# A router on unnormed, transposed half blocks, and a first index taken before the softmax

## The chip, the cores and the metric

The kernel runs on one core of a Trainium2 chip. The metric is the device time of one execution in microseconds (us). Before the change it was 1559.31 us, the median of three runs (1558.9 to 1561.21).

## The reference, cut to what matters

One layer of an encoder: 512 tokens of width 1024, two attention branches, an output projection, and a mixture of 32 experts of which each token uses four. All of it is float32. The part that the change touches:

```
x  = x + merged @ w_out
h2 = x * rsqrt(mean(x*x) + eps) * g_ffn
logits = h2 @ w_router + b_router            # (512, 32)
top_vals, top_idx = top_k(logits, 4);  gate = softmax(top_vals)
# each expert: rows h2[tokens of e]; gu = rows @ w_gate_up[e] + b; clamped SwiGLU; @ w_down[e] + b; times gate
x  = x + sum over the experts;  out = rmsnorm(x) * g_final
```

## The kernel before, in words

There is no planner: each engine runs a list of instructions written out by hand, in order, and waits on semaphores. A product in float32 is made of three float32r products: each operand is split into a rounded part ("hi", copied by ScalarE, ACT) and the rest ("lo", subtracted by VectorE, DVE), and TensorE (PE) multiplies hi by hi, hi by lo and lo by hi (L1446 to L1448, one 128x512 product each). The router alone multiplies in plain float32.

**Output projection.** `out_part(n, j)` is six products of quarter `j` of the depth for half block `n`; half block `n` is 512 columns of token block `n // 2`. Half blocks 0 to 3 go through together, then 4 to 7 one after the other. `residual(n)` (L1231, DVE) adds a half block to `xs`. `root(c)` (L890 to L892, ACT) starts the store of block `c` of `xs` to memory, squares it, and takes the root; `norm(c)` (L1237, L1238, DVE) writes the normed block to `xn2`, and `store_rows(c)` (ACT's queue) stores that as rows to gather from.

**Routing.** `h2_transpose` (L1650, PE) turns eight 128x128 tiles of the normed block, ACT and DVE copy four each out of PSUM (`h2T_half` L872, `h2_out` L1245), `router` (L1660, PE) makes the logits. `choose(c)` (L1251 to L1259, DVE) finds the top four and the mask. From the masks PE counts positions (L1686, L1689), DVE makes `posx` (L1307, L1309). `softmax` (L1266 to L1273, DVE) makes the gates in three bfloat16 parts. `serve(n)` (L1318, DVE) writes the one-hot matrix of expert `n`, `slots(n)` (L1701, PE) multiplies it with index and gates, `index(n)` (L931 to L939, ACT) turns that into row numbers and gates, and GpSimd (POOL) gathers the 128 rows (L618). `rows_in` (L1708, PE) transposes them, and ACT (`rows_hi`, L943) and DVE (`rows_lo`, L1324) split them into `XT`.

**Experts.** An expert has twelve 1 MB chunks of weights. For chunk `c`, ACT copies hi (`first_split_hi` L883 or `ex_split_hi` L879), DVE subtracts lo (`ex_split_lo` L1279), PE runs twelve products (`weigh`). Chunks 0 to 3 (gate) of the first expert come ahead of the loop; then each turn of the loop runs chunks 4, 5, `slots` and `rows_in` for later experts, 6, 7, then 0, 1 of the next expert, the transposes of the hidden rows (L1716), 2, 3, and 8 to 11. `sigmoid` (L969, ACT, behind a table load at L972) and `glu` (L1358, DVE) come once per expert; `serve` for the next expert stands behind `glu`. SyncE (SP) issues the loads of chunks, each when its place is free. In the first expert it loads chunks 4 to 7 when the output projection is done, and 8 to 11 when the first gather has landed:

```
sp.wait_ge(wout_ps, 2 * NT)
sp.dma_start(bd[:, :], b_down[0]).then_inc(bd_in, 16)
for c in range(4, 8):
    load_expert(sp, c, 0)
```

## Time and profile before

| what | value |
|---|---|
| median of three runs | 1559.31 us |
| the profiled execution | 1559.76 us, of it the span 1558.0 us |
| PE, DVE, ACT, POOL busy | 97%, 84%, 70%, 17% of the span |
| chain that ended last | PE 93%, DVE 3%, ACT 2%, issue 1% |
| granted TensorE clock, mean | 0.986 |
| DMA over the span | 477.36 MB, mean 306 GB/s |

Busy time is what the hardware profiler recorded of one execution. An engine's idle time costs something only where another engine's last work waits for it; the chain of waits, followed back from the last instruction, tells which engine that is.

### The profile page before, as it was taken

Reading aid. Unit: us, or ns where it says so; the run is one execution under the profiler, and the core shown is the slowest. Engines: PE = TensorE matmul, PEld = TensorE weight load, DVE = VectorE, ACT = ScalarE, POOL = GpSimd, SP = SyncE. Lnnn points to the kernel's source line nnn. Section 1 sums busy time; section 2 is a strip of 40 time slices with the busy share of each in tenths; the row PEclk is TensorE's granted clock in tenths of the full one; section 3 lists DMA queues with packets and bytes.
Section 4 is the critical chain, followed back from the end, with each engine's and each line's share of the span. In section 5 each row is a group of like instructions: output and inputs, shape, how many; then the busy total and the mean of one; then the engine's idle time right before and its main releaser. Section 6 shows DMA issues by size and latency. Waiting matters only on the chain.

```text
span 1558.0 us, 21230 instructions
## 1 busy us (share of the span) xinstructions
PE 1512.6 (97%) x7254; PEld 1240.9 (80%) x7287; DVE 1311.9 (84%) x1021; ACT 1091.1 (70%) x1158; POOL 268.3 (17%) x164
## 2 busy tenths in 40 slices
PE   7999999997999999999999999999999999999997
PEld 6888788886788888888888888888888888888884
DVE  4556587656899999999999999999999999999975
ACT  4344587424787777877777787787777778778772
POOL 6302144100001110111100001202120022002211
PEclk9999999998899999999999999999999999999997
DMA  8330001545999999999999999999999999999972
GB/s 299 122 100 36 1 1 55 200 141 181 378 363 391 385 389 385 379 391 379 375 387 386 386 387 381 388 390 385 376 372 391 386 378 394 387 387 380 388 263 113
DMA packets 131102, 477.36 MB, mean 306 GB/s; under 512 B 9720, under 2 KB 10240, under 8 KB 130976
## 3 DMA queue, kind: packets, MB, share of 16 engines
q1 hardware_dynamic: 117536, 434.79, 72.1%
q0 software_dynamic: 9936, 36.44, 9.1%
q10 hardware_dynamic: 3600, 5.73, 1.1%
q8 instruction: 18, 0.29, 0.1%
q14 instruction: 12, 0.10, 0.0%
HBM read 452.81 MB, written 24.12 MB: 306 GB/s over the span
## 4 chain that ended last, share of the span: by engine, by line
PE 93%; DVE 3%; ACT 2%; issue 1%; DMA 0%; ACTq 0%; SPq 0%; DVEq 0%
PE ps L1446 28%; PE ps L1447 28%; PE ps L1448 28%; PE ps L1708 2%; PE ps L1716 2%; PE ps L1735 2%; PE ps L1494 1%; PE ps L1537 1%; DVE pT_lo L1155 1%; PE ps L1538 0%; ACT probs L754 0%; PE ps L1479 0%; DMA xs<-in_x 0%; DVE split L1068 0%; PE ps L1515 0%
## 5 line engine op out<-in xcount | busy, mean ns | idle before, releaser
L1279 DVE TENSOR_TENSOR chunk_lo<-chunk,chunk_hi 128x2048 fp32r<-128x2048 f32 x384 | 859.3, 2285 | 39.0 <-ACT chunk_hi L879 36.0
L879 ACT ACTIVATE chunk_hi<-chunk 128x2048 fp32r<-128x2048 f32 x378 | 722.6, 1914 | 109.2 <-PE ps L1448 108.1
L1446 PE MATMUL ps<-chunk_hi,XT 128*128 128x512 f32 x1024 | 404.8, 395 | 2.0 <-DVE XT L1324 2.0
L1448 PE MATMUL ps<-chunk_hi,XT 128*128 128x512 f32 x1024 | 400.0, 391 | 0.0
L1447 PE MATMUL ps<-chunk_lo,XT 128*128 128x512 f32 x1024 | 399.9, 391 | 0.0
L644 POOL DMA_INDIRECT sum_rows<-y,idx x31 | 116.4, 3755 | 921.7 <-ACT y L985 833.8
L1446 PEld LDWEIGHTS ps<-chunk_hi,XT 128*128 128x128 f32 x1024 | 192.8, 188 | 41.1 <-DVE XT L1324 2.4
L1448 PEld LDWEIGHTS ps<-chunk_hi,XT 128*128 128x128 f32 x1024 | 192.4, 188 | 40.4
L1447 PEld LDWEIGHTS ps<-chunk_lo,XT 128*128 128x128 f32 x1024 | 192.8, 188 | 38.9
L1446 PE MATMUL ps<-chunk_hi,hidT 128*128 128x512 f32 x512 | 200.4, 391 | 0.0
L1448 PE MATMUL ps<-chunk_hi,hidT 128*128 128x512 f32 x512 | 200.1, 391 | 0.0
L1447 PE MATMUL ps<-chunk_lo,hidT 128*128 128x512 f32 x512 | 200.1, 391 | 0.0
L1446 PEld LDWEIGHTS ps<-chunk_hi,hidT 128*128 128x128 f32 x512 | 96.8, 189 | 21.6 <-issue 1.4
L1447 PEld LDWEIGHTS ps<-chunk_lo,hidT 128*128 128x128 f32 x512 | 96.8, 189 | 20.2
L1448 PEld LDWEIGHTS ps<-chunk_hi,hidT 128*128 128x128 f32 x512 | 96.7, 189 | 20.2
L943 ACT ACTIVATE XT<-ps 128x512 fp32r<-128x512 f32 x64 | 38.2, 599 | 79.3 <-PE ps L1708 54.9
L1068 DVE TENSOR_TENSOR split<-raw,split 128x2048 fp32r<-128x2048 f32 x14 | 37.2, 2660 | 54.2 <-ACT split L694 54.2
L618 POOL DMA_INDIRECT xg<-h_rows,idx x34 | 46.1, 1357 | 150.7 <-ACT idx L937 106.0
L1382 DVE TENSOR_SCALAR hid<-ps 128x1024 f32<-128x1024 f32 x32 | 39.2, 1224 | 29.3 <-PE ps L1448 29.3
L1446 PE MATMUL ps<-hT,split 128*128 128x512 f32 x128 | 50.2, 392 | 0.0
L1448 PE MATMUL ps<-hT,split 128*128 128x512 f32 x128 | 49.9, 390 | 0.0
L754 ACT ACTIVATE probs<-ps,negm 128x512 f32<-128x512 f32 (+2 forms) x64 | 39.4, 616 | 14.9 <-DVE negm L1161 14.5
(272 smaller groups left out, 1900.7 us busy)
## 6 DMA issues: line engine op xcount, KB each, us to landing
chunk<-in_w_gate_up SPq DMA_DIRECT2D x256, 1024.0 KB, 8.8
chunk<-in_w_down SPq DMA_DIRECT2D x128, 1024.0 KB, 7.1
raw<-in_w_in SPq DMA_DIRECT2D x14, 1024.0 KB, 6.8
xs<-in_x SPq DMA_DIRECT2D x8, 512.0 KB, 5.2
w_out<-in_w_out SPq DMA_DIRECT2D x4, 1024.0 KB, 6.8
raw<-in_w_branch_a SPq DMA_DIRECT2D x2, 1024.0 KB, 6.0
raw<-in_w_branch_b SPq DMA_DIRECT2D x2, 1024.0 KB, 6.9
sum_rows<-xs ACTq DMA_DIRECT2D x4, 512.0 KB, 2.6
```

Of the source, the lines that this page charges most:

```text
L618: g.indirect_dma_start(out=xg, out_offset=None, in_=h2buf, in_offset=bass.IndirectOffsetOnAxis(ap=idx[:, col:col + 1], axis=0)).then_inc(g ...
L644: g.indirect_dma_start(out=acc, out_offset=bass.IndirectOffsetOnAxis(ap=idx[:, u:u + 1], axis=0), in_=ysb, in_offset=None, compute_op=ALU. ...
L754: a.activation(probs[:, j % 2, n, 0:w], ps[:, i % 3, 0:w], ACT.Exp, bias=negm[:, j % 2, n:n + 1], accum_out=psum_p[:, j % 2, n:n + 1]).the ...
L879: a.activation(chunk_hi[hi_slot(c, nxt)][:, :], chunk[c][:, :], ACT.Copy).then_inc(ex_hi, 1)
L943: a.activation(XT[:, 0, 4 * half:4 * half + 4, :].rearrange("p k n -> p (k n)"), ps[:, 6 + half, 0:4 * CAP], ACT.Copy).then_inc(xt_hi, 1)
L1068: v.tensor_tensor(split[:, n % NIN_SPLIT, 1, :], raw[:, n % NIN, :], split[:, n % NIN_SPLIT, 0, :].bitcast(F32), ALU.subtract).then_inc(in ...
L1279: v.tensor_tensor(chunk_lo[c][:, :], chunk[c][:, :], chunk_hi[hi_slot(c, nxt, first)][:, :].bitcast(F32), ALU.subtract).then_inc(ex_lo, 1)
L1382: v.tensor_scalar(hid, ps[0:CAP, 2:4, :].rearrange("p t n -> p (t n)"), 8.0, -6.0, ALU.min, ALU.max).then_inc(clip_ready, 1)
L1446: mm(dst, lhsT(0), rhs(0), start=start, stop=False)
L1447: mm(dst, lhsT(0), rhs(1), start=False, stop=False)
L1448: return mm(dst, lhsT(1), rhs(0), start=False, stop=stop)
L1708: last = t_.transpose(ps[:, 6 + k // 4, (k % 4) * CAP:(k % 4 + 1) * CAP], xg[:, k * 128:(k + 1) * 128], ident[0:CAP, 0:CAP])
```

## The change

The router multiplies the unnormed sums `xs`, transposed in half blocks of 512 columns (`x1T`, four places), with router weights that DVE has multiplied once by `g_ffn`; the factor 1/rms of a token is put on the logits in `choose`. The half transposes and half routers stand between the quarter products of half blocks 4 to 7. On ACT the stores of `xs` come behind the roots, and the square of the last block is taken in two halves. The first expert's index is made from a product with two columns (index and one), ahead of the softmax of all four blocks, its gates later by a second product. `slots(2)`, the third expert's index product, stands behind `weigh` of chunk 2, and ACT's `index(2)` behind the splitting of the gathered rows and of chunk 3. The gathered rows are split half by half. On SP, chunks 4 and 5 are loaded behind the output projection, the bias table and chunks 6 to 11 when all rows are stored, and `b_down` last.

```diff
 # SP
             sp.wait_ge(wout_ps, 2 * NT)
-            sp.dma_start(bd[:, :], b_down[0]).then_inc(bd_in, 16)
-            for c in range(4, 8):
-                load_expert(sp, c, 0)
+            load_expert(sp, 4, 0)
+            load_expert(sp, 5, 0)
+            sp.wait_ge(rows_stored, 2 * NT * 16)
             sp.wait_ge(scattered, ADDED)
             sp.dma_start(bias_tab[:, :], bias_parts).then_inc(bias_back, 16)
-            sp.wait_ge(gathered, 16)
-            for c in range(8, 12):
+            for c in range(6, 12):
+                if c == 8:
+                    sp.wait_ge(logits_ps, 2 * NT)
                 load_expert(sp, c, 0)
+            sp.dma_start(bd[:, :], b_down[0]).then_inc(bd_in, 16)
 # ACT
+            act.dma_start(g16[8:16, :], g_ffn.rearrange("l (k p) -> (l k) p", p=128)).then_inc(g_mix_in, 16)
...
+            root(0)
+            store_sums(0)
+            root(1)
+            store_sums(1)
+            x1T_out(0)
+            x1T_out(2)
             store_rows(0)
             store_rows(1)
             act.wait_ge(branch_ps, KD)
             first_split_hi(0)
+            root(2)
+            x1T_out(4)
+            store_sums(2)
+            store_rows(2)
+            half_square(0)
...
+            x1T_out(6)
+            half_square(1)
...
+            store_sums(3)
+            store_rows(3)
             a.activation(warm[:, :], eps[:, :], ACT.Exp)
+            for c in range(NT):
+                top_exp(c)
...
+            act.wait_ge(idx_first, 1)
+            a.activation(f5[:, 0:2], ps[0:CAP, 5, 440:442], ACT.Copy).then_inc(f2_ready, 1)
...
+            a.activation(idx[:, 0:1], f5[:, 0:1], ACT.Identity, bias=s1[:, 0:1]).then_inc(idx_ready, 1)
+            first_split_hi(1)
+            act.wait_ge(idx_done, 1)
...
             act.wait_ge(gates_set, 1)
             index(1, slice(1, 2))
+            act.wait_ge(wout_ps, 2 * NT)
+            first_split_hi(2)
             act.wait_ge(gateT_ps, 1)
             a.activation(gateT[:, :], ps[0:E, 3, :], ACT.Copy).then_inc(gateT_out, 1)
+            act.wait_ge(xt_first, 1)
+            a.activation(XT[:, 0, 0:4, :].rearrange("p k n -> p (k n)"), ps[:, 6, 0:4 * CAP], ACT.Copy).then_inc(xt_hi, 1)
+            rows_hi(1, 1)
+            first_split_hi(3)
+            act.wait_ge(gates_set, 2)
+            index(2, slice(2, 3))
             act.wait_ge(rows_stored, 2 * NT * 16)
             first_split_hi(4)
             first_split_hi(5)
 # DVE
+            dve.wait_ge(late_in, 32)
+            v.tensor_tensor(wr[:, :, :], wr[:, :, :], gcol[:, KD:2 * KD].unsqueeze(2).to_broadcast([128, KD, E]),
+                            ALU.mult).then_inc(wr_scaled, 1)
             for n in range(4):
                 residual(n)
             norm(0)
+            x1T_copy(1)
             norm(1)
+            x1T_copy(3)
+            choose(0)
             residual(4)
+            ex_split_lo(0, 0, first=True)
+            choose(1)
             residual(5)
             norm(2)
+            x1T_copy(5)
             residual(6)
+            choose(2)
             residual(7)
+            x1T_copy(7)
             norm(3)
             choose(3)
...
             serve(0)
+            softmax(0, NT)
+            dve.wait_ge(idx_done, 1)
+            serve(1)
+            ex_split_lo(0, 1, first=True)
+            ex_split_lo(0, 2, first=True)
+            rows_lo(1, 0)
+            rows_lo(1, 1)
+            ex_split_lo(0, 3, first=True)
...
             dve.wait_ge(idx_done, 2)
             serve(2)
 # PE
+            def x1_transpose(n):
+                pe.wait_ge(x1_ready, n + 1)
+                if n >= 2:
+                    pe.wait_ge(x1T_odd if n % 2 else x1T_even, n // 2)
+                for k in range(4):
+                    at = n % 2 * 512 + k * 128
+                    last = t_.transpose(ps[:, n % 2, k * 128:(k + 1) * 128], xs[:, n // 2, at:at + 128], ident[:, :])
+                last.then_inc(x1T_ps, 1)
...
+            out_part(5, 3)
+            out_part(6, 0)
+            router(4)
+            out_part(6, 1)
+            x1_transpose(5)
+            out_part(6, 2)
+            out_part(6, 3)
+            router(5)
+            out_part(7, 0)
+            out_part(7, 1)
+            x1_transpose(6)
+            out_part(7, 2)
+            out_part(7, 3)
+            router(6)
+            x1_transpose(7)
             pe.wait_ge(wout_ps, 2 * NT)
             pe.sem_inc(ex_used, 2)
+            router(7)
...
+            pe.wait_ge(gathered, 16)
+            for k in range(KD):
...
+                if k == 3:
+                    last.then_inc(xt_first, 1)
+            last.then_inc(xt_ps, 1)
             for c in range(4):
+                if c % 2 == 0:
+                    pe.wait_ge(xt_lo, c // 2 + 1)
...
                 weigh(c, c, c, XT, 0, c == 0, c == 3).then_inc(ex_used, 1)
+                if c == 2:
+                    slots(2)
+            pe.wait_ge(f5_ready, 3)
```

## Rows read from the trace of the kernel before

**Rows 1.** Busy time by stretch: engines in order, then PEclk, DMA share, GB/s.

```profile
core 0: us, PE busy (x) PEld busy (x) DVE busy (x) ACT busy (x) POOL busy (x), PEclk, DMA share, GB/s
369.00:396.00 27.00, 12.50 (x112) 11.05 (x111) 21.60 (x61) 15.87 (x33) 3.52 (x2) 0.67 0.78 278
484.00:520.00 36.00, 35.93 (x171) 29.47 (x171) 33.74 (x20) 28.41 (x25) 6.33 (x3) 1.00 1.02 387
```

**Rows 2.** Timeline of PE: start us, us, line, operation, count, [idle before, releaser].

```profile
343.68 0.39 PE L1446 MATMUL ps<-w_out_hi,merged_T_hi 128*128 128x512 f32 x1
...
354.56 1.03 PE L1650 MATMUL ps<-ident,xn_a 128*128 128x128 f32 x8
355.35 0.48 PE L1446 MATMUL ps<-w_out_hi,merged_T_hi 128*128 128x512 f32 x1
...
360.93 1.86 PE L1660 MATMUL ps<-w_router,h2T 128*128 128x32 f32 x16
...
395.91 0.80 PE L1446 MATMUL ps<-chunk_hi,XT 128*128 128x512 f32 x1 [2.01 <-DVE XT L1324]
...
405.78 0.38 PE L1735 MATMUL ps<-bias_tab,pick 128*128 128x512 bf16 x1
...
414.18 0.26 PE L1701 MATMUL ps<-feats,shared 128*128 x4
```

**Rows 3.** Timeline of ACT, the same columns.

```profile
355.86 1.06 ACT L890 ACTIVATE xn_b<-xs 128x1024 f32<-128x1024 f32 x1 [9.40 <-DVE xs L1231]
357.24 0.58 ACT L872 ACTIVATE h2T<-ps 128x512 f32<-128x512 f32 x1
...
384.66 0.28 ACT L937 ACTIVATE idx<-f,s 128x1 int32<-128x1 f32 x1
...
391.60 0.28 ACT L939 ACTIVATE gates<-f,s 128x1 f32<-128x1 f32 x1
...
395.39 3.70 ACT L883 ACTIVATE chunk_hi<-chunk 128x2048 fp32r<-128x2048 f32 x2
...
405.03 1.28 ACT L972 ACT_TABLE_LOAD   x1
...
408.93 1.03 ACT L969 ACTIVATE sig<-ps 128x1024 f32<-128x1024 f32 x1 [2.41 <-PE ps L1448]
```

**Rows 4.** Timeline of DVE, the same columns.

```profile
369.21 0.69 DVE L1231 TENSOR_TENSOR xs<-xs,ps 128x512 f32<-128x512 f32 x1 [0.74 <-PE ps L1448]
...
378.71 0.19 DVE L1251 TENSOR_TENSOR lg<-ps,brt 128x32 f32<-128x32 f32 x1
...
379.72 0.18 DVE L1259 TENSOR_SCALAR mask<-repl 128x32 bf16<-128x32 f32 x1
...
380.86 0.18 DVE L1266 TENSOR_TENSOR shared<-shared,mask 128x32 f32<-128x32 f32 x1
...
382.92 0.69 DVE L1318 TENSOR_TENSOR shared<-iota_all,shared 128x512 bf16<-128x512 f32 x1
...
397.31 4.49 DVE L1279 TENSOR_TENSOR chunk_lo<-chunk,chunk_hi 128x2048 fp32r<-128x2048 f32 x2 [1.46 <-ACT chunk_hi L883]
...
409.99 1.23 DVE L1358 TENSOR_TENSOR sig<-ps,sig 128x1024 f32<-128x1024 f32 x1 [2.66 <-ACT sig L969]
411.13 0.68 DVE L1318 TENSOR_TENSOR shared<-iota_all,shared 128x512 bf16 x1
```

**Rows 5.** Timeline of POOL: the first gather.

```profile
385.83 2.56 POOL L618 DMA_INDIRECT xg<-h_rows,idx  x1 [106.01 <-ACT idx L937]
```

**Rows 6.** DMA issues at 358.88, 373.33, 385.83 and 394.70 us: count, KB, us to landing.

```profile
h_rows<-xn_b ACTq DMA_DIRECT2D x1, 512.0 KB, 2.6
...
h_rows<-xn_b ACTq DMA_DIRECT2D x1, 512.0 KB, 9.3
...
xg<-h_rows,idx POOLq DMA_INDIRECT x1, 5.9
...
xg<-h_rows,idx POOLq DMA_INDIRECT x1, 8.3
```

**Rows 7.** Waits over the whole span: us in total, times, longest.

```profile
PE ps L1458 <- DVE gcol L1060: 4.2, 1, 4.2
```

More of the change, by code:

```diff
@@ L306, in encoder_block @@
         sums_ready = sem("sums_ready")
-        acc_in = [sem(f"acc_in{c}") for c in range(NT)]
         gfin_in = sem("gfin_in")
@@ L865, in _, with x1T_out @@
             wo_split_hi(3)
-            def h2T_half(c):
-                act.wait_ge(h2T_ps, c + 1)
-                if c >= 2:
-                    act.wait_ge(logits_ps, c - 1)
-                a.activation(h2T[:, c % 2, 0:4, :], ps[:, 0, :].rearrange("p (k n) -> p k n", n=128),
-                             ACT.Copy).then_inc(h2T_a, 1)
+            def x1T_out(n):
+                act.wait_ge(x1T_ps, n + 1)
+                if n >= 4:
+                    act.wait_ge(logits_ps, n - 3)
+                a.activation(x1T[:, n % 4, :, :], ps[:, 0, :].rearrange("p (k n) -> p k n", n=128),
+                             ACT.Copy).then_inc(x1T_even, 1)
             def ex_split_hi(i, c, nxt=True):
@@ L1309, in _ @@
             v.tensor_scalar(posx[:, :, :], posx[:, :, :], -1024.0, None, ALU.add).then_inc(route_ready, 1)
-            softmax(3, 4)
             dve.wait_ge(route_ready, 1)
@@ L1343, in _ @@
             v.tensor_copy(items_i[:, 0:1], npass[:, :]).then_inc(items_ready, 1)
-            dve.wait_ge(idx_done, 1)
-            serve(1)
-            for c in range(1, 3):
-                ex_split_lo(0, c, first=True)
             dve.wait_ge(idx_done, 2)
             serve(2)
-            ex_split_lo(0, 3, first=True)
-            rows_lo(1, 0)
-            rows_lo(1, 1)
             dve.wait_ge(items_ready, 1)
@@ L1642, in out_half, with router @@
                     out_part(n, j)
-            def h2_transpose(c):
-                pe.wait_ge(xn2_ready, c + 1)
-                if c:
-                    pe.wait_ge(h2T_a, c)
-                    pe.wait_ge(h2T_d, c)
-                for k in range(KD):
-                    last = t_.transpose(ps[:, k // 4, (k % 4) * 128:(k % 4 + 1) * 128],
-                                        xn2[c][:, k * 128:(k + 1) * 128], ident[:, :])
-                last.then_inc(h2T_ps, 1)
-            def router(c):
-                pe.wait_ge(h2T_a, c + 1)
-                pe.wait_ge(h2T_d, c + 1)
-                if c >= 2:
+            def x1_transpose(n):
[6 more added lines that the diff above has]
+                last.then_inc(x1T_ps, 1)
+            def router(n):
+                c = n // 2
+                pe.wait_ge(x1T_odd if n % 2 else x1T_even, n // 2 + 1)
+                if n == 0:
+                    pe.wait_ge(wr_scaled, 1)
+                if c >= 2 and n % 2 == 0:
                     pe.wait_ge(lg_ready, c - 1)
-                for k in range(KD):
-                    last = mm(ps[:, 2 + c % 2, c * E:(c + 1) * E], h2T[:, c % 2, k, :], wr[:, k, :],
-                              start=(k == 0), stop=(k == KD - 1))
+                for k in range(4):
+                    last = mm(ps[:, 2 + c % 2, c * E:(c + 1) * E], x1T[:, n % 4, k, :], wr[:, n % 2 * 4 + k, :],
+                              start=(n % 2 == 0 and k == 0), stop=(n % 2 == 1 and k == 3))
                 last.then_inc(logits_ps, 1)
@@ L1736, in add_bias @@
                        bias_tab[:, col:col + 512], start=start, stop=False)
-            slots(0)
+            pe.wait_ge(onehot_ready, 1)
+            for c in range(NT):
+                last = mm(ps[0:CAP, 5, 440:442], onehot[:, c, :], feats[:, c, 0, 0:2], start=(c == 0), stop=(c == NT - 1))
+            last.then_inc(idx_first, 1)
+            pe.wait_ge(f2_ready, 1)
+            pe.wait_ge(gates_known, 1)
+            for c in range(NT):
+                last = mm(ps[0:CAP, 5, 450:453], onehot[:, c, :], feats[:, c, 0, 2:5], start=(c == 0), stop=(c == NT - 1))
+            last.then_inc(idx_done, 1)
             slots(1)
-            slots(2)
             for c in range(NT):
```

135 lines of the change are left out of this document (66 added, 69 removed).

## The prediction

> **What bounds the kernel now.** I read the busy times by stretch first [rows 1]. In the expert loop PE is busy 35.93 of 36 us, DVE 33.74 and ACT 28.41, at full clock: there PE is the bound, and the loop ends when it started plus a fixed amount. Between 369 and 396 us PE is busy 12.50 of 27 us at a mean clock of 0.67: this is the gap between the output projection and the first expert. So I read the timelines of the engines there, from the end of the last output product (DVE adds it at 369.21 [rows 4], so it ended at 369.2) to the first expert product at 395.91 [rows 2]. Two points decide the time: when PE starts the first expert (called S, 395.91), and whether it then runs without a stop. Before, it does: chunk 3 is reached at 405.78 (its bias product), `slots(3)` at 414.18 [rows 2], which is S + 18.3, with no idle note on either.
>
> **Start-up and weights.** The second tiny load for `g_ffn` comes behind the first. The product it delays is needed by a wait of PE that DVE ends, 4.2 us long [rows 7], so it has room: 0, at most 0.6 if that room is gone. Scaling the router weights is one DVE operation before its first residual, with DVE idle: 0.
>
> **The output projection gets longer.** From 343.68 [rows 2] come 16 quarters of six products; successive products start 0.227 us apart, so 96 x 0.227 = 21.8. Before, 3.5 us of other work stand between them, which gives 343.7 + 21.8 + 3.5 + 0.2 (tail of the last) = 369.2. After, seven half transposes and six half routers stand between them. A block of eight transposes takes 0.8 (354.56 to 355.35), and the product behind it costs 0.1 more (0.48 against 0.39) [rows 2]: 0.5 for a half, 3.5 in all. A whole router shows 1.86, of which 1.7 until the next work can start: 0.9 for a half with its change-over, 5.4 in all. And `router(4)` has a wait: ACT runs `root(2)` ahead of `x1T_out(4)`, and the root needs half block 5 added. From the start of that square to the end of the copy behind it took 355.86 to 357.82 [rows 3], 2.0; with 0.8 for the addition ahead (0.69 [rows 4] and a hop) it is 2.8 after the end of half block 5, and PE has only one quarter, 1.36, to fill it: 1.5 us standing. The last output product then ends at 343.7 + 21.8 + 3.5 + 5.4 + 1.5 + 0.2 = 376.1, 6.9 later. Bounds of this term: 4.5 (no wait, free change-overs) and 8.
>
> **The index comes sooner after it.** From 376.1: addition 0.7, half transpose 0.6, DVE's copy 0.7 (378.1); then `norm(3)` 1.4 on DVE, under which `router(7)` hides (379.5); `choose` from 378.71 to 379.90 [rows 4], 1.2 (380.7); mask to `posx` done, 379.90 to 380.95, 1.05 less the overlap with what came next, so 1.1 (381.8); the one-hot matrix 0.7 (382.5). The 2.0 us of `softmax(3, 4)` from 380.86 to 382.92 [rows 4] are gone from here. Index product and ACT's three operations: from the end of the matrix, 383.61, to the end of the index, 384.94 [rows 3, 4], 1.3. The index is there at 383.8, 1.1 us sooner than before. Of about 8 us saved behind the last product, 6.9 were spent ahead of it.
>
> **Gather.** POOL began 0.9 after the index (385.83 [rows 5]): 384.7 at best. But POOL, and SP's further loads, also wait until all rows are stored. The last store goes out behind `norm(3)`, at 379.6. The same store landed in 2.6 us alone and in 9.3 beside four chunk loads [rows 6]. Here two chunks, issued at 376, and the store of the sums stand beside it. I take 5, the middle: stored at 384.6, gather at 385.2, between 384.7 and 389.5. The gather took 5.9 us when nothing ran beside it and 8.3 beside chunk loads [rows 6]. After the change SP issues the bias table and six chunks at the same moment that frees the gather, so it is the second kind: I take 7.8 and keep 5.9 as the low end, landing at 393.0. Before it landed at 391.7. From landing to the first product it was 4.2 (391.7 to 395.91 [rows 2]); split half by half it is four transposes at the low clock 1.2, ACT 0.6, DVE 0.7, hops 0.2 = 2.7. So S becomes 395.7, 0.2 earlier; bounds -2.7 (384.7 + 5.9 + 2.7) and +4.6 (389.5 + 8.3 + 2.7).
>
> By *DMA: Bandwidth & Descriptors* of the Trainium skill, section "Queues, rings and completion order", an engine takes turns between the queues that have work. Equal turns would add to the gather only its own 0.52 MB once more, some 1.3 us at 400 GB/s, so 7.2 in place of 7.8 and a sum 0.6 lower; the trace's 8.3 is above that.
>
> **The third index now holds up ACT.** This is the term that counts. Before, ACT made all three indices before the rows were split (gates of the third done at 391.88) and copied chunks 4 and 5 at 395.39 [rows 3], at S - 0.5. After, `slots(2)` stands behind chunk 2 on PE, and `index(2)` on ACT ahead of the copies of 4 to 7. Counted from S: chunk 3 was reached at 405.78, S + 9.9 [rows 2], so `slots(2)` is done at S + 10.1. ACT's five small operations take 1.2, up to 391.88 [rows 3]: S + 11.3. ACT's copy of chunk 4 takes 1.9 (3.70 for two [rows 3]) and DVE's difference 2.3 (4.49 for two [rows 4]): S + 15.5. PE has finished chunk 3 at S + 13.3. **First stop, 2.2 us.** Then chunks 4 and 5, 5.4 us, to S + 21.0.
> ACT meanwhile copies 5, 6, 7 at 1.8 each, to S + 18.6, loads a table for 1.28, warms it for 0.2, and runs the sigmoid, 1.03 [rows 3]: S + 21.1. DVE's differences, 2.2 apart, hold it to S + 22.1; `glu` 1.23 and `serve(3)` 0.68 follow, overlapping by 0.1 each [rows 4]: S + 23.9. PE needs that for `slots(3)`. **Second stop, 2.9 us.** Before, `serve(3)` was done at 411.81, 2.4 us ahead of PE. Then 1.3 of small work and chunks 6, 7 bring PE to S + 30.7; DVE, with three differences and half of the next rows behind `serve(3)`, is ready at S + 31.1: **third stop, 0.4**. With `slots(2)` itself, 0.3, that is 5.9. After that DVE's 33.7 of 36 us per expert [rows 1] is again below PE's. Bounds: 5.0 if hand-overs are tighter, 7.5 if the clock falls in a stop. It stood at 0.67 over 369 to 396 [rows 1], and the first six products took 2.73 (395.91 to the full rate) in place of 1.36.
>
> **The sum.** -0.2 + 5.9 = +5.7, on the profiled execution's 1559.76 (span 1558.0 and 1.76 around it): 1565.5. That execution is 0.45 above the median of the three runs, so for the median I say 1565.2. Moving `b_down` costs nothing: it is needed at the last expert. The two half squares cost ACT 0.5 us while DVE adds and copies.
>
> **Rivals.**
> - *The first expert really starts early.* The stores land in 3 us, the gather in 5.9: S - 2.7, stops as above: +3.2, 1562.7. For it: only two chunks are in flight. Against: SP's loads are released together with the gather. Chance 0.15.
> - *Stores and gather collide.* The store takes its 9.3, the gather 8.3: S at 400, +4.6 + 5.9, 1569.6. Against: half the chunk traffic of before. Chance 0.08.
> - *The half blocks are nearly free*, no stop at `router(4)` and free change-overs: index 2.4 sooner, stores too, S at 393.3, and the stops at their low end of 5.0: +2.4, 1561.5, which is within 0.2%. For it: ACT idled 9.40 us ahead of its square [rows 3]. Against: the queue of ACT puts the root first. Chance 0.12.
> - *The loads pace the loop, and the end comes sooner.* DMA is at 1.02 of its share and 387 GB/s in the loop [rows 1]. If the end is set by when the last chunk can be loaded, SP's release of chunks 8 to 11, until now only after the gather (391.7), comes at 384.6 to 388: about 4 us sooner, and PE's stops cost nothing because it would have waited for chunks anyway: 1555.5. It decides if PE's idle time in the loop is ended by loads. Against: PE is idle 0.07 of 36 us there [rows 1], so loads pace nothing. Chance 0.10.
>
> My forecast has 0.55, with a range of its own of 1562.4 to 1568.5.
>
> **Numbers.** About 0.2%, 3.1 us, is what a measurement of this kernel can tell from no change: up to 1562.4 it is "same". Slower: nearly all of the forecast (0.52), half of the first rival (0.08), the second (0.08), a third of the third (0.04): 0.72. Faster: the last rival, 0.10. Same: 0.18. The range, 1560.8 to 1569.0, leaves out the last rival, the end of the second and little else.
>
> **What would show it.** In the profile after: the last output product ends at 376, with a stop of 1.5 us before `router(4)`; index at 383.8; gather issued near 385 and landed near 393; first expert product at 395.7; a stop of some 2 us of PE that DVE's `chunk_lo` ends and one of some 3 us that DVE's one-hot matrix ends, and none before the second expert's end beyond that; ACT idle for about 8 us before it makes the third index. It would be wrong if ACT's copies of chunks 4 to 7 ran ahead of PE, if the first product came before 393, or if PE waited in the loop for loads.

## The result, and the profile after

The changed kernel takes 1577.73 us, the median of five runs (1574.27 to 1596.65). The kernel before, timed beside it, took 1560.83 us (1558.9 to 1561.49, five runs). The ratio is 1.0117, with a 95% interval of 1.0087 to 1.0147. So the change costs 1.2%, some 17 us by the medians. Ratios, here and below, are of the runs within 1.5% of the fastest of their kernel; medians and ranges are of all runs. The prediction had 1565.2 and a range up to 1569.0: the direction was right, the size was a third of what came.

The profiled execution is the slowest of the five: 1596.65 us, span 1594.9, against 1558.0. This matters for reading it: 36.9 us are to be explained in this trace, while the median run has less than half of that. First the busy time by stretch of the kernel after, where the second row covers the first expert from its fourth chunk on and the start of the second, and the last one a stretch of the loop.

```profile
core 0: us, PE busy (x) PEld busy (x) DVE busy (x) ACT busy (x) POOL busy (x), PEclk, DMA share, GB/s
369.00:396.00 27.00, 12.08 (x94) 10.05 (x93) 14.56 (x34) 11.78 (x27) 1.05 (x1) 0.72 0.56 180
...
415.00:450.00 35.00, 31.75 (x141) 25.59 (x143) 34.97 (x21) 31.58 (x27) 4.31 (x1) 0.95 0.93 338
484.00:520.00 36.00, 35.30 (x167) 28.71 (x167) 32.64 (x20) 27.17 (x25) 8.03 (x2) 1.00 1.02 382
```

In the gap between the output projection and the first expert DVE was busy 21.60 of 27 us before [rows 1] and is busy 14.56 now. The last 10.93 us before the first rows are a wait for DMA, whose share over the gap is 0.56 against 0.78. From 415 to 450 PE has lost 3.2 us (it was busy 34.93 there before). In the loop it is busy 35.30 of 36 us, not 35.93.

The timeline of PE, with the places that the prediction named:

```profile
363.23 1.08 PE L1695 MATMUL ps<-w_router,x1T 128*128 128x32 f32 x8 [1.41 <-ACT x1T L880]
...
375.46 0.39 PE L1482 MATMUL ps<-w_out_hi,merged_T_lo 128*128 128x512 f32 x1
...
398.99 1.94 PE L1811 MATMUL ps<-ident,xg 128*128 128x128 f32 x8 [10.93 <-DMA xg<-h_rows,idx]
401.49 0.80 PE L1480 MATMUL ps<-chunk_hi,XT 128*128 128x512 f32 x1 [0.56 <-DVE XT L1357]
...
416.97 0.50 PE L1480 MATMUL ps<-chunk_hi,XT 128*128 128x512 f32 x1 [2.25 <-DVE chunk_lo L1311]
...
425.56 0.56 PE L1756 MATMUL ps<-feats,shared 128*128 x4 [1.21 <-DVE shared L1351]
```

The stop ahead of `router(4)`, the last output product (ended at 375.85) and both stops of the first expert are where they were expected. But S, the first expert product, is at 401.49 and not at 395.7. PE stood 10.93 us, and the gather released it. ACT and POOL show when the gather could start:

```profile
383.31 0.29 ACT L976 ACTIVATE idx<-f,s 128x1 int32<-128x1 f32 x1
...
411.63 0.18 ACT L950 ACTIVATE f<-ps 128x5 f32<-128x5 f32 x1 [8.27 <-PE ps L1756]
```

```profile
389.46 1.05 POOL L625 DMA_INDIRECT xg<-h_rows,idx  x1 [109.77 <-DMA h_rows<-xn_b]
```

The index was there at 383.6, 1.3 us sooner than before (384.94 [rows 3]). POOL began the gather at 389.46, 3.6 us later than before (385.83 [rows 5]), and its releaser is no longer ACT's index but the store of the rows. The DMA issues of this stretch, in microseconds to landing, say why:

```profile
chunk<-in_w_gate_up SPq DMA_DIRECT2D x2, 1024.0 KB, 10.0
sum_rows<-xs ACTq DMA_DIRECT2D x1, 512.0 KB, 9.6
...
h_rows<-xn_b ACTq DMA_DIRECT2D x1, 512.0 KB, 9.7
...
xg<-h_rows,idx POOLq DMA_INDIRECT x1, 9.4
```

The last store of rows, issued at 379.44, landed 9.7 us later, beside two chunk loads issued at 375.88, when the output projection ended. The gather, issued at 389.46 beside the bias table and chunks issued from 389.20 on, then took 9.4. What each queue moved meanwhile (packets, MB, share of the 16 DMA engines) tells where the time went. By what they move, q1 is SP's queue, q10 ACT's and q0 POOL's. For the stores, 378 to 382 us and 384 to 388:

```profile
q1 hardware_dynamic: 223, 0.88, 86.2%
...
q10 hardware_dynamic: 238, 0.85, 52.1%
q1 hardware_dynamic: 118, 0.42, 26.0%
```

For the gather, 390 to 395 us:

```profile
q1 hardware_dynamic: 353, 1.38, 91.4%
q0 software_dynamic: 11, 0.05, 3.0%
```

ACT's queue had a store of sums issued at 377.37 and the store of rows, and moved nothing up to 382; afterwards the two queues shared. The gather moved 0.05 of its 0.52 MB in its first 5 us. So most of the delay is not slow sharing but a late start behind the load that was issued first.

In the loop ACT waits at its copy of the index product for the last scatter, that is for the store of an expert's results, because `index` overwrites one of four places (waits from the first to the last turns: us in total, times, longest):

```profile
ACT f L950 <- DMA sum_rows<-y,idx: 75.4, 28, 5.6
PE ps L1771 <- ACT f L950: 20.8, 14, 2.6
```

The same wait in the kernel before:

```profile
ACT f L931 <- DMA sum_rows<-y,idx: 23.3, 27, 1.8
```

PE had no such wait before. All of it sits in turns like the first of the following two; the second shows a turn of the same trace that isn't slow:

```profile
642.78 6.24 POOL L651 DMA_INDIRECT sum_rows<-y,idx  x1 [28.60 <-ACT y L1019]
...
1052.96 2.62 POOL L651 DMA_INDIRECT sum_rows<-y,idx  x1 [30.97 <-ACT y L1019]
```

```profile
658.38 0.18 ACT L950 ACTIVATE f<-ps 128x5 f32<-128x5 f32 x1 [4.96 <-DMA sum_rows<-y,idx]
```

```profile
658.80 1.06 PE L1771 MATMUL ps<-ident,hid 128*128 128x128 f32 x8 [1.93 <-ACT f L950]
```

Where POOL is at the scatter for 2.62 us, the scatter lands some 12 us after its start and ACT waits about 1.3. Where it takes 6.24, it lands after 15.5 and PE stands 1.9. A turn takes 35.47 us in the first case, and 36.3 to 39.8 in fourteen successive turns of the second.

To put the 36.9 us together I cut every trace at the same four points: S, the start of the first scatter, the start of the last, and the end. The last stretch goes with the clock that the last expert was granted: it took 44.9, 47.4 to 47.7 or 49.0 us, at a mean granted clock of 1.00, 0.90 or 0.86 over 35 us of it. The changed kernel itself had 47.4 in one trace and 44.9 in another. So I take it as no term of the sum, but it blurs single executions by some 2 us to either side.

| trace | S | S to first scatter | first to last scatter | to the end | span |
|---|---|---|---|---|---|
| before | 395.91 | 52.6 | 1062.1 | 47.4 | 1558.0 |
| after | 401.49 | 58.85 | 1087.15 | 47.4 | 1594.9 |

That gives +5.6 for the start, +6.25 for the first expert and +25.1 for slow turns of the loop. The experiments take these three apart.

### The profile page after: what moved, and what is told of

Read it like the earlier page. It is cut to its first block, busy times and chain, and to the rows that moved or that the text cites. A ratio compares the mean times of both kernels' runs of the same rounds, so it can differ in the third digit from the quotient of the medians.

```text
span 1594.9 us, 21237 instructions
## 1 busy us (share of the span) xinstructions
PE 1519.3 (95%) x7258; PEld 1241.3 (78%) x7291; DVE 1308.3 (82%) x1013; ACT 1088.7 (68%) x1162; POOL 302.2 (19%) x164
## 4 chain that ended last, share of the span: by engine, by line
PE 58%; DMA 14%; DVE 1%; issue 1%; ACT 1%; ACTq 0%; DVEq 0%; POOLq 0%
PE ps L1480 18%; PE ps L1481 18%; PE ps L1482 18%; DMA sum_rows<-y,idx 13%; PE ps L1771 2%; PE ps L1763 1%; PE ps L1790 1%; DMA xg<-h_rows,idx 1%; DVE chunk_lo L1311 0%; PE ps L1834 0%; DVE fin L1460 0%; ACT y L1019 0%; ACT f L950 0%; DVE fin L1451 0%; ACT fin_sq L1071 0%
## 5 line engine op out<-in xcount | busy, mean ns | idle before, releaser
L651 POOL DMA_INDIRECT sum_rows<-y,idx x31 | 142.4, 4592 | 912.9 <-ACT y L1019 828.3
L625 POOL DMA_INDIRECT xg<-h_rows,idx x34 | 54.0, 1589 | 162.7 <-DMA h_rows<-xn_b 109.8
L1364 DVE TENSOR_TENSOR hidT<-ps,hidT 128x1024 fp32r<-128x1024 f32 x32 | 39.2, 1224 | 54.7 <-ACT hidT L967 54.6
L950 ACT ACTIVATE f<-ps 128x5 f32<-128x5 f32 x33 | 5.8, 176 | 84.0 <-DMA sum_rows<-y,idx 75.4
L1771 PE MATMUL ps<-ident,hid 128*128 128x128 f32 x256 | 33.7, 275 | 21.6 <-ACT f L950 20.8
```

What stands on the lines that cost most here:

```text
L625: g.indirect_dma_start(out=xg, out_offset=None, in_=h2buf, in_offset=bass.IndirectOffsetOnAxis(ap=idx[:, col:col + 1], axis=0)).then_inc(g ...
L651: g.indirect_dma_start(out=acc, out_offset=bass.IndirectOffsetOnAxis(ap=idx[:, u:u + 1], axis=0), in_=ysb, in_offset=None, compute_op=ALU. ...
L1364: v.tensor_tensor(hidT[:, 1, :, :].rearrange("p (t k) n -> p t (k n)", t=2), ps[:, 6:8, 0:4 * CAP], hidT[:, 0, :, :].rearrange("p (t k) n ...
L1771: last = t_.transpose(ps[:, 6 + k // 4, (k % 4) * CAP:(k % 4 + 1) * CAP], hid[:, k * 128:(k + 1) * 128], ident[0:CAP, 0:CAP])
```

## The experiments

The theory has four parts: (a) the chunk loads issued at the end of the output projection hold up the last stores, (b) the loads released with the gather hold up the gather, (c) the late third index stops PE in the first expert, (d) slow turns come on top in some executions, from ACT's wait for the scatter. The rivals stand in the expectations.

### Undoing one part at a time

**index3_back**: the changed kernel with the third index at its old place.

```diff
 # PE
             slots(1)
+            slots(2)
...
-                if c == 2:
-                    slots(2)
 # ACT
+            act.wait_ge(gates_set, 2)
+            index(2, slice(2, 3))
             act.wait_ge(gateT_ps, 1)
...
             first_split_hi(3)
-            act.wait_ge(gates_set, 2)
-            index(2, slice(2, 3))
 # DVE
             ex_split_lo(0, 1, first=True)
+            dve.wait_ge(idx_done, 2)
+            serve(2)
```

> The changed kernel with one part undone: the third expert's index product, its one-hot matrix and ACT's five operations stand ahead of the split of the gathered rows again. Theory A (the three stops of PE in the first expert, 5.9 us, come from the late third index, and the slow turns of the expert loop come from the lag that these stops leave on DVE): chunk 4 is reached without a stop, PE waits nowhere in the loop, and the time is the changed kernel's 1571 without slow turns less 5.9, 1565 to 1566, in every run alike. Rival B (the slow turns come from loads that start late): the stops go, but scatters still land after 15 us in many turns and the time stays at 1568 to 1572 with a spread of some us.

**stores_first**: chunks 4 and 5 are loaded only when all rows are stored.

```diff
+            sp.wait_ge(rows_stored, 2 * NT * 16)
             load_expert(sp, 4, 0)
             load_expert(sp, 5, 0)
-            sp.wait_ge(rows_stored, 2 * NT * 16)
```

> The changed kernel with the loads of chunks 4 and 5 moved behind the stores of the rows. Theory A (the last store of rows is held up by these two loads, 9.2 us in place of 2.6, and holds the first gather): the store lands within 4 us, the gather is issued at 384 to 385 in place of 389.5, the first expert product is 4 to 5 us sooner, 396.5 to 397.5, and the time is 4 to 5 us lower than the changed kernel's on the same turns of the loop. Rival B (the store is slow for another reason, such as the store of the sums ahead of it on the same queue): the gather moves by less than 2 us.

**gather_alone**: the bias table and chunks 6 to 11 wait for the gather.

```diff
             sp.wait_ge(scattered, ADDED)
+            sp.wait_ge(gathered, 16)
             sp.dma_start(bias_tab[:, :], bias_parts).then_inc(bias_back, 16)
```

> The changed kernel with the bias table and chunks 6 to 11 loaded only when the first gather has landed, as chunks 8 to 11 were before the change. Theory A (the loads released at the same moment take the gather from 5.9 to 9.4 us): the gather lands 5.6 to 6.5 us after its issue, the first expert product comes 3 to 3.5 us sooner. Against that, chunks 6 and 7 land later; if that is on the path, PE waits for chunk 6 at about 18 us after its first expert product. Rival B (the gather takes 9 us for a reason of its own): it stays at 9 us and the time rises or stays.

**late_index3_only**: the kernel before, with `slots(2)` behind chunk 2 and `index(2)` at the end of ACT's list ahead of the copies of chunks 4 to 7.

```diff
 # PE
-            slots(2)
...
                 weigh(c, c, c, XT, 0, c == 0, c == 3).then_inc(ex_used, 1)
+                if c == 2:
+                    slots(2)
 # ACT
-            index(2, slice(2, 3))
             rows_hi(1, 0)
             rows_hi(1, 1)
...
             a.activation(gateT[:, :], ps[0:E, 3, :], ACT.Copy).then_inc(gateT_out, 1)
+            index(2, slice(2, 3))
```

> The kernel before with one part of the change alone: the third index product behind chunk 2 on PE, and ACT's third index behind the split of the first rows. Theory A: the first expert product stays at 396, PE then stops 2.2 us at chunk 4, 2.9 us at the fourth one-hot matrix and 0.4 us at the second expert's first chunk, 5.5 to 6 us in all, and because the lag of DVE is the same as in the changed kernel some turns of the loop are slow too: 1566 to 1580, with a spread. Rival B (slow turns come from the late start of the loads, not from this): 1565 to 1566 in every run, no scatter above 12.5 us.

These four ran on one chip, and the kernel before, beside them, spread from 1559.77 to 1593.18 us (median 1565.68). The medians were 1569.74, 1569.37, 1579.70 and 1567.93, the ratios 1.0039 (0.9977 to 1.0101), 1.0021 (0.9955 to 1.0086), 1.0108 (1.0035 to 1.0181) and 1.0013 (0.9954 to 1.0072). The times alone decide little; the cuts of the traces do:

| trace | gather starts | S | S to first scatter | first to last scatter |
|---|---|---|---|---|
| before | 385.83 | 395.91 | 52.6 | 1062.1 |
| after | 389.46 | 401.49 | 58.85 | 1087.15 |
| index3_back | 390.11 | 402.43 | 53.5 | 1074.1 |
| stores_first | 384.56 | 396.15 | 60.8 | 1062.1 |
| gather_alone | 390.81 | 397.93 | 61.9 | 1065.8 |
| late_index3_only | 388.55 | 398.56 | 61.6 | 1062.1 |

(a) holds. In stores_first (its last output product within 0.1 us of the changed kernel's) the store landed in 3.0 us, and the gather started with the index as its releaser again:

```profile
384.56 1.05 POOL L625 DMA_INDIRECT xg<-h_rows,idx  x1 [104.79 <-ACT idx L976]
```

Its two stops in the first expert stayed; they belong to (c):

```profile
412.15 0.50 PE L1480 MATMUL ps<-chunk_hi,XT 128*128 128x512 f32 x1 [2.25 <-DVE chunk_lo L1311]
...
420.74 0.56 PE L1756 MATMUL ps<-feats,shared 128*128 x4 [2.81 <-DVE shared L1351]
```

(b) holds as well. In gather_alone the gather took 4.5 us in place of 9.4 (in stores_first 9.0, beside the loads), and S came 3.6 us sooner though the gather started 1.35 later. But it didn't pay. In its first expert the second stop was 2.82 us, not 1.21, and the later chunks cost one more, of 0.99; a slow turn cost 3.7 and the clock of the last stretch 1.6 on top. Of the 3.0 us that its first expert lost against the changed kernel's trace only the 0.99 is shown to come from the later chunks: with the loads as in the changed kernel, idx8_after below needs 61.9 too.

```profile
xg<-h_rows,idx POOLq DMA_INDIRECT x1, 4.5
```

The stop that the later chunks cost:

```profile
432.20 0.49 PE L1481 MATMUL ps<-chunk_hi,XT 128*128 128x512 f32 x1 [0.99 <-DVE XT L1358]
```

(c) holds from both sides. With the third index back, the first expert has no stop and takes 53.5 us; the late index alone, in the kernel before, costs two stops there, 2.19 and 2.81 us, and 9.0 us up to the first scatter. Its trace also reached S 2.65 us later than the kernel before, where I had expected no difference: there the routers of the last block ran at the low clock (3.60 us for sixteen products, before 1.94; mean granted clock over 376 to 378 us 0.50, before 1.00). Its median is not slower by that much, and its lowest run, 1563.08, is 3.3 above the lowest of the kernel before. Those runs have no trace, so whether they lose less in the first expert stays open.

(d) can't be priced from these. Six turns of index3_back are slow (36.6 us and more), one of gather_alone and none of the other two, which fits none of the parts undone. My expectation for index3_back, 1565 to 1566 in every run without slow turns, failed with that, and the slow turns expected of late_index3_only did not show in its trace. Single executions without a trace went to 1593.18 (before), 1594.29 (gather_alone) and 1601.50 (stores_first).

### Taking the loop's wait away

ACT waits for the scatter because the fourth index overwrites the place that the scatter reads. With eight places, instead of four, the wait isn't needed, and slow turns should go. The edit also unrolls POOL's loop by eight in place of four. Short form, in the kernel before (**idx8_before**) and the changed one (**idx8_after**):

```diff
-        idx = sb("idx", [CAP, 4], I32)
-        gates = sb("gates", [CAP, 4])
+        idx = sb("idx", [CAP, 8], I32)
+        gates = sb("gates", [CAP, 8])
...
-                    act.wait_ge(scattered, 16 * i + ADDED)
-                    index(i + 3, bass.ds((i + 3) % 4, 1))
+                    index(i + 3, bass.ds((i + 3) % 8, 1))
```

> The kernel before with eight columns for row numbers and gates in place of four, POOL's loop unrolled by eight, and ACT's wait for the last scatter ahead of each index product taken out, since the column it writes has been free for four experts. Theory A (slow turns of the expert loop: ACT waits up to 5.6 us for a scatter whose descriptors POOL took 6.2 us to write, PE then waits about 2 us at the hidden rows' transposes, and ACT starts the next turn late again): with the wait gone no turn is over 35.6 us whatever POOL takes; every run is at 1558 to 1561, while the kernel before beside it spreads up to 1593. Rival B (the scatters are slow because the loads or the chip are slow, and PE's wait is only where it shows): the spread stays, and PE waits elsewhere, for chunks or for rows.

> The changed kernel with the same edit. Theory A: what is left of the change is the later first expert product (5.6 us) and the stops in the first expert (5.9 to 6.5, with a fall of the clock up to 8): 1570 to 1573 in every run, no slow turns. Rival B: 1574 to 1597 as before, since the late loads cause the slow turns.

**all_four** is the changed kernel with the three undone parts together, and `x1T_out(4)` ahead of `root(2)`; **best** is the same with eight places.

```diff
 # ACT
-            root(2)
             x1T_out(4)
+            root(2)
```

> As the one with all repairs, but with four columns and ACT's wait for the scatter. Theory A: the same 1555 to 1557 in its best run, with slow turns on top in some executions, so a spread of 2 to 30 us. Rival B (the slow turns belong to the stops of the changed kernel): no spread.

> The changed kernel with all repairs: third index early, loads of chunks 4 and 5 behind the stores, the bias table and chunks 6 to 11 behind the gather, the copy of the half transposes ahead of the root on ACT, and the eight columns. Theory A: last output product at 374.4, index at 382.3, rows stored by 382.5, gather issued at 383.3 and landed 5 to 7 us later, first expert product at 391 to 393, 3 to 5 us sooner than before the change, no stops: 1555 to 1557 in every run. Rival B (the loads that now start at 389 are behind, and PE waits for chunks in the second expert): some of it is given back and the time is 1558 to 1562.

These four ran together; the kernel before beside them had a median of 1561.57 (15 runs, 1558.21 to 1615.25).

| kernel | median (range) | ratio (interval) | S | S to first scatter | first to last scatter |
|---|---|---|---|---|---|
| idx8_before | 1560.68 (1557.88 to 1563.07, 10 runs) | 0.9994 (0.9982 to 1.0006) | 396.25 | 52.7 | 1062.1 |
| idx8_after | 1574.73 (1573.31 to 1575.08, 4) | 1.0087 (1.0066 to 1.0109) | 402.77 | 61.9 | 1062.1 |
| all_four | 1570.83 (1568.85 to 1573.27, 4) | 1.0067 (1.0041 to 1.0092) | 392.69 | 64.9 | 1062.1 |
| best | 1571.39 (1568.82 to 1572.44, 5) | 1.0062 (1.0043 to 1.0080) | 393.49 | 65.5 | 1062.1 |

With eight places no trace has a slow turn, and the ten and four runs lie within 5.2 and 1.8 us, where the kernel before went to 1615.25 on the same chip. The slow turns of the traces are a wait of PE for ACT's wait, so without the second the first can't come. But they are rare: all_four, which keeps ACT's wait, has none in its trace and lies within 4.4 us too (I had expected a spread), and the edit changed POOL's loop as well. So that the wait is needed for them is likely, not proven. They don't seem to be a product of the change either: 1615.25 is a run of the kernel before, at a mean granted clock of 0.987 that is as high as in its fast runs, though without a trace. The gain in the usual run is nothing (0.9994). What is left between idx8_after and idx8_before is the change's own cost: 14.0 us by the medians, 13.1 by the spans.

The traces of idx8_after and of the changed kernel show one thing more. Both stop PE for 1.41 us ahead of `router(4)`. In idx8_after the granted clock then fell to the lower of its two levels (1.2 GHz, for 2.4), in the changed kernel it didn't; here are the four microseconds from 364.5 in both, the changed kernel first:

```profile
364.50:368.50 4.00, 4.00 (x21) 3.30 (x20) 0.69 (x1) 0.00 (x0) 0.00 (x0) 1.00 0.35 139
```

```profile
364.50:368.50 4.00, 4.00 (x14) 3.18 (x14) 0.69 (x1) 0.00 (x0) 0.00 (x0) 0.57 0.33 131
```

From the first half transpose to the last output product it was 32.1 us in three traces where the clock fell (idx8_after, gather_alone, idx8_index3_back) and 30.5 in the four others with that stop: 1.6 us more for the same stop. With `x1T_out(4)` ahead of `root(2)` the stop is gone, and it is 28.9 in all four traces.

best and all_four were to be faster than the kernel before and are 0.6% slower, and the miss is instructive. S did come 2.4 to 3.2 us ahead of the kernel before's. But the bias table and chunks 6 to 11 now waited for the gather, behind chunks 4 and 5 that were issued only at 380.08, and the second expert's first chunks stand in the same queue behind them. Here are ACT and PE of best:

```profile
417.56 1.91 ACT L888 ACTIVATE chunk_hi<-chunk 128x2048 fp32r<-128x2048 f32 x1 [9.89 <-DMA chunk<-in_w_gate_up]
```

```profile
428.92 0.79 PE L1480 MATMUL ps<-chunk_hi,XT 128*128 128x512 f32 x1 [9.97 <-DVE XT L1357]
```

PE stands 10 us in one place. A load that is kept out of the way of a store has to be issued earlier, not later.

### The loads issued earlier

**loads_earlier** keeps the third index early, `x1T_out(4)` first and eight places, and issues chunks 4 and 5 when half block 6 has been transposed, some 3 us ahead of the end of the output projection (at 369.94, with the last output product at 372.29). **loads_split** also keeps chunks 8 to 11 behind the gather (the last line of the diff).

```diff
-            sp.wait_ge(wout_ps, 2 * NT)
+            sp.wait_ge(x1T_ps, 7)
             load_expert(sp, 4, 0)
             load_expert(sp, 5, 0)
+            sp.wait_ge(wout_ps, 2 * NT)
             sp.wait_ge(rows_stored, 2 * NT * 16)
...
                 if c == 8:
                     sp.wait_ge(logits_ps, 2 * NT)
+                    sp.wait_ge(gathered, 16)
```

> After the change, with the third index early again, x1T_out(4) ahead of root(2), eight index columns (no wait of ACT in the loop), and chunks 4 and 5 loaded when half block 6 has been transposed instead of behind the output projection. My theory (the loads of chunks 4 and 5 hold up the last stores, the load of all the rest together holds up the gather, the late third index stops PE): the two chunks are issued near 372 and land before the last stores go out, the stores land in 3 to 4 us, the gather is issued near 382.5, takes 9 beside the loads, S is 394.2, PE has no stop in the first expert and none for chunks in the second, first scatter S + 53, the loop 1062.1: span 1556.5, 1558.3 for the median, 1 to 3 us under the kernel before. Rival (chunks 4 and 5 now collide with the stores of block 2 and the loads only shift the delay): S stays at 396 or later, median 1560.5 or more. Second rival (the kernel after loses its time elsewhere, in the routers between the quarters): the last output product stays past 376 and the median is over 1563.

> The same, and chunks 8 to 11 wait for the first gather to land, so only the bias table and chunks 6 and 7 run beside the gather. My theory: the gather takes 7 to 8.5 us in place of 9, S 393.5; chunks 8 to 11 are issued near 391, as in the kernel before (391.7), and are needed at the end of the first expert, so no stop: median 1557.5, within 1 us of loads_earlier. Rival (loads that come late are paid for in the second expert, as where bias table and chunks 6 to 11 all waited for the gather: PE stood 10 us there): a stop of 2 to 6 us behind the first expert, median 1560 to 1564.

**idx8_index3_back** is idx8_after with the edit of index3_back, and **again** the changed kernel as it was.

> The changed kernel with eight index columns and the third index made early again (slots(2) behind slots(1), index(2) ahead of the gate copies, serve(2) behind chunk 1's difference). Beside the changed kernel with eight columns alone (span 1571.6, median 1574.7) this prices the late third index alone, in a loop that ACT does not hold up. My theory: the three stops and the low clock in them go, from S to the first scatter 53 in place of 61.9: span 1562.5 to 1563.5, median near 1565, and the first product still near 402 (S unchanged, since stores and gather are as in the changed kernel). Rival (the stops are set by the late start of the gather and its loads, not by the place of the index): the time from S to the first scatter stays at 59 or more and the median at 1572 or more.

> The changed kernel unchanged, beside the others on the same chip. My theory: 13 us over the kernel before for certain (start and stops), near 1574, plus up to 21 us more in runs whose loop has slow turns, where ACT waits for the last scatter with POOL's descriptor writing at 6.2 us in place of 2.6 or 4.8: runs between 1574 and 1597, and in the profile of one with time T the loop from first to last scatter is longer than 1062.1 by about T less 1574. Rival (the slow turns belong to one placement of the program or one chip, and do not come again): all runs within 3 us of 1574.

Beside them the kernel before had a median of 1561.93 (21 runs, 1558.48 to 1565.09).

| kernel | median (range) | ratio (interval) | gather starts | S | S to first scatter |
|---|---|---|---|---|---|
| loads_earlier | 1563.79 (1559.05 to 1566.40, 10 runs) | 1.0010 (0.9996 to 1.0023) | 383.29 | 397.51 | 52.9 |
| loads_split | 1563.18 (1559.55 to 1566.16, 10) | 1.0007 (0.9997 to 1.0016) | 385.23 | 397.39 | 53.5 |
| idx8_index3_back | 1569.09 (1567.94 to 1570.29, 4) | 1.0043 (1.0026 to 1.0059) | 389.04 | 401.07 | 54.0 |
| again | 1574.19 (1567.43 to 1585.10, 6) | 1.0084 (1.0056 to 1.0113) | 388.10 | 399.96 | 58.8 |

idx8_index3_back prices the late third index: 5.6 us against idx8_after by the medians (ratios 1.0043 and 1.0087, which gives 6.9), and the stops are gone from the trace. I had expected 1565 for it, since I took the 9 us that a trace loses between S and the first scatter for the price of the index. loads_earlier is another 5.3 us lower by the medians, but it undoes two things. In the traces, its output projection is 3.3 us shorter than in idx8_index3_back, which is `x1T_out(4)` and the clock behind its stop, and from the last output product to S it gains only 0.85; loads_split gains 3.1 there. So most of the 5.3 is the stop ahead of `router(4)`, and no run changes the time of the loads alone. With both, the change is back to within a thousandth of the kernel before, and PE has no stop in the first two experts. My expectation of 1 to 3 us under the kernel before failed, on two numbers. The stores took 6.3 and 6.7 us, not 3 to 4, since the two chunks were still landing (11.0). And the gather took 11.6 in loads_earlier:

```profile
383.29 3.00 POOL L626 DMA_INDIRECT xg<-h_rows,idx  x1 [105.09 <-DMA h_rows<-xn_b]
```

```profile
xg<-h_rows,idx POOLq DMA_INDIRECT x1, 11.6
```

POOL stood 3.00 us on it, not 1.05. In loads_split it was 1.05 again, and the gather took 9.5, though only the bias table and two chunks stood beside it instead of the bias table and six. So what stands at the head of SP's queue when the gather is issued makes it slow, not what comes behind, which fits the late start of the gather in the trace after the change; and the rival to loads_split, a stop in the second expert, did not come.

again: four of six runs between 1571.10 and 1574.55, one at 1585.10, and the profiled one at 1567.43. That one had no slow turn, ran its last expert at full clock (44.9 us from the last scatter, 2.5 less than in the first trace), and its output projection had ended 1.3 us sooner. The rival, that slow turns belonged to one chip, isn't borne out for 1585.10, but this run has no trace of its own. 1567.43 is 6.6 us under the 1574 that I took as the lower end: the tail's clock and the phase of the start are 4 us of spread that I hadn't allowed for. Most of the rest is clock as well: idx8_after, at 1573.31, lost 1.6 us behind the stop of `router(4)` and 3.1 in the first expert that this trace did not lose.

No version here is faster than the kernel before by more than can be measured.

## Why the prediction was wrong, step by step

- **The output projection gets longer: right.** 6.9 us forecast, the last product at 376.1; measured 375.85, with a stop of 1.41 ahead of `router(4)` (1.5 forecast). Where the clock fell behind that stop it was 1.6 more, which the sum did not have.
- **The index comes sooner: right.** 383.8 forecast, 383.6 measured.
- **Gather: this is the term that failed**, "I take 5, the middle: stored at 384.6, gather at 385.2", and "7.8" for the gather. Measured: 9.7 for the store and 389.46 for the start of the gather; 9.4 for the gather. That is 4.3 and 1.6, together the 5.8 us by which S was missed (401.49 against 395.7), since landing to first product was right (2.6 for 2.7). The 5 was not even the middle, which is 6.0. The bounds had both: 9.3 for a store beside loads, 8.3 for a gather beside loads [rows 6]; the rival "stores and gather collide", with S at 400, was the one that came, and I had given it 0.08 with the argument "half the chunk traffic of before". stores_first shows that the chunk loads are the cause (3.0 in place of 9.7), and gather_alone shows it for the gather (4.5 in place of 9.4). The argument failed because the amount wasn't what counted. Two chunks issued 3.6 us ahead of the store delayed it (9.7) as much as four issued 3.7 us ahead had (9.3), two issued 6.3 us ahead less (6.7 and 6.5), and in loads_split the bias table and two chunks delayed the gather as much as the table and six. By the Trainium skill's *DMA: Bandwidth & Descriptors*, section "Queues, rings and completion order", an engine takes turns between queues that have work; the 7.2 us that equal turns gave for the gather is 2.2 below the 9.4 measured. The trace agrees with turns only for the second half: in its first 5 us the gather moved 0.05 MB against SP's 1.38, and only then the queues shared (0.48 against 0.96 MB from 395 to 399). That late start is what the sum lacked; why a queue starts late no run here shows.
- **The third index holds up ACT: right in place, in part too small in size.** "First stop, 2.2 us": 2.25 at the forecast place, S + 13.2. "Second stop, 2.9": 2.92 in idx8_after and 2.81 or 2.82 in three others; 1.21 and 1.20 in the changed kernel's two traces, where the clock fell after the first stop, so that chunks 4 and 5 took longer and filled the wait. The third stop, 0.4, came in none but gather_alone. The term of 5.9 (5.0 to 7.5) came out as 6.2 in those two traces, and as 8.2 to 9.3, above its upper bound, in the four others with the late index (stores_first, late_index3_only, idx8_after, gather_alone). By the medians of idx8_after and idx8_index3_back it is 5.6; from S to the first scatter those two traces differ by 7.9. What exceeds the two stops is PE at the low clock behind them (in idx8_after the mean granted clock over 415 to 450 is 0.95, in the kernel before 1.00) and at the start: the sum had the stops and, but for its upper bound, not the clock.
- **Loop unchanged: wrong in this trace, right in the usual run.** I priced only what PE's bound gives and took one run's loop for the loop. ACT's wait for the scatter was in the trace of before (27 times, up to 1.8 us), and I did not read how near it was to PE: ACT behind it feeds PE's transposes of the hidden rows. Once POOL is at the scatter for 6.2 us instead of 2.6 or 4.8, PE stands, and in the first trace this lasted for fourteen turns. This is the 25 us of that trace. The median of those five runs is 3 us above idx8_after's, so in the usual run it is a small part at most.
- **The sum.** By idx8_after against idx8_before, without slow turns, the change costs 14.0 us by the medians. Forecast 5.7. The spans differ by 13.1: S +6.5, the first expert +9.2, the last stretch -2.6 by its clock. The forecast's direction came from the late third index, which is 5.6 of the 14.0. Of the S +6.5, the last output product is 7.5 later (1.6 of it the clock behind the stop of `router(4)`), and the stretch from the last output product to S gains only 1.0: I had 6.9 spent and 7.1 gained there, and the wait for DMA took most of the difference. loads_earlier, with the loads ahead and `x1T_out(4)` first, takes back 5.3 of the 14.0.
- **Where the index's gain went.** Nothing could use it. Even at 3 us for the store the gather started at 384.56, 1.3 us sooner than before, and then took 9.0 beside loads.

## What to carry to other kernels

Here a transfer on the critical path was slow as soon as a bulk load had been issued shortly ahead of it, and two chunks did as much as four: where the trace of before has the same transfer beside loads, take that number, not the middle of it and the quiet one. Issue the load early; holding it back until the transfer has landed cost 10 us here. An index that is made sooner brings nothing while the data that it points to is still being stored, so follow every condition of the waiting engine to its last. A stop of PE costs more than its length where the granted clock falls behind it: give the term a second price for that. And before a loop is called unchanged, look for waits in it that end a little ahead of the bound: such a wait cost nothing in the usual execution and 25 us in one.

## What the runs showed of the hardware that was not expected

- POOL's time at a scatter is mostly one of three sizes, 2.6, 4.8 and 6.2 us. In the slow turns they come one after another (fifteen scatters of 5.9 to 6.25 in a row, then 2.6 for most), so a slow turn seems to bring the next. In a slow turn DVE's three differences were back to back from 1.9 us ahead of the scatter (640.86, 6.69 us), in a fast one from 3.3 us ahead (1049.63, 6.69 us). The Trainium skill, *SBUF — State Buffer*, section "Who interferes with whom", says that a VectorE instruction with two SBUF inputs contends with GpSimd where that reads SBUF. It would fit a phase between the two engines that keeps itself; no run here moved the one against the other, so it stays open.
- The last expert's clock: 47.4 us at a mean granted clock of 0.90, 44.9 at 1.00 and 49.0 at 0.86, for the same work. It is a spread of 4 us in single executions, and the changed kernel, run twice, shows 2.5 of it.
- The same stop of 1.41 us ahead of `router(4)` was followed by some 4 us at a mean granted clock of 0.6 in three of seven traces, and by none in four.
- A store or gather issued shortly behind a bulk load of another queue moved next to nothing for about 5 us (in the changed kernel's trace ACT's store of sums from 377.37 to 382, the gather from 389.46 to 394), and then shared with it.
- The time at the low clock at the first expert's start varied as well: over the first 10 us from S the mean granted clock was 0.70 in idx8_after and 0.84 in the changed kernel's trace.
